# Operand sums of the output product made per head inside the memory attention, and one gate unit placed ahead of the spread of the key norms

## What is computed

```
# first stack, layers l = 0 and 1: attention to a memory of 256 rows, 4 heads of 256
q = rmsnorm(x, xa_ln[l]) @ xa_wq[l]
k = rmsnorm(mem, xa_mem_ln[l]) @ xa_wk[l]
v = rmsnorm(mem, xa_mem_ln[l]) @ xa_wv[l]
o = softmax(q @ k.T / 16) @ v            # per head
x = x + o @ xa_wo[l]

# second stack, layers A0 and A1: sliding window attention, 16 query heads and 4 key heads of 64
q, k, v, z = split(u @ a_w_in)
q = rope(rmsnorm_2(q, q_gain), pos)      # norms per head of 64
k = rope(rmsnorm_2(k, k_gain), pos)
o = window_attention(q, k, v, sinks)
y = (o * silu(z)) @ a_w_out
```

## Time and profile before

| what | value |
|---|---|
| median of 3 runs | 3629.98 us (3616.33 to 3632.56) |
| profiled execution, its own time | 3631.66 us |
| its span in the profile | 3629.8 us |
| mean granted TensorE clock | 0.976 of full |
| TensorE busy (matmuls) | 3461.8 us, 95% |
| VectorE busy | 1997.6 us, 55% |
| ScalarE busy | 716.1 us, 20% |
| GpSimd busy | 84.5 us, 2% |
| memory attention, layers mem0 and mem1 | about 523 to 555 and 1523 to 1555 us |
| gate stretch of the sliding layers | about 2099 to 2162 and 3432 to 3496 us |

### The profile page before, as it was taken

The page is one execution under the profiler, slowest core; times in us unless marked ns, Lnnn a source line. Parts: engine busy times, 40 slices in busy tenths (PEclk is TensorE's granted clock), DMA queues, the critical chain, the costliest instruction groups (busy, mean ns, idle before and its releaser), DMA issues.

```text
span 3629.8 us, 43978 instructions
## 1 busy us (share of the span) xinstructions
PE 3461.8 (95%) x16715; PEld 2727.9 (75%) x16715; DVE 1997.6 (55%) x4671; ACT 716.1 (20%) x1763; POOL 84.5 (2%) x100
## 2 busy tenths in 40 slices
PE   8987999999999999999999898999999999999988
PEld 3365688888854558888888765888887888887766
DVE  4353167554413783675544658644354656557566
ACT  2221011110012560111100125012212111121143
POOL 0000000000000000000000011000000000000110
PEclk9988999999999999999999999999999999999999
DMA  3100322222211003212222130222211222102311
GB/s 129 49 21 12 111 74 70 82 93 82 105 58 47 13 19 112 80 70 82 93 82 93 59 94 14 92 70 76 73 65 45 95 80 86 43 24 83 110 43 47
DMA packets 39367, 251.98 MB, mean 69 GB/s; under 512 B 5708, under 2 KB 5836, under 8 KB 11008
## 3 DMA queue, kind: packets, MB, share of 16 engines
q1 hardware_dynamic: 31616, 224.41, 17.5%
q10 hardware_dynamic: 4496, 11.89, 1.2%
q0 software_dynamic: 3056, 12.96, 1.1%
HBM read 240.58 MB, written 2.16 MB: 67 GB/s over the span
## 4 chain that ended last, share of the span: by engine, by line
PE 88%; DVE 8%; issue 2%; ACT 1%; DMA 1%; ACTq 0%; POOL 0%; POOLq 0%; DVEq 0%
PE PL L1213 26%; PE PX L1213 20%; PE PL L921 14%; PE PL L1561 4%; PE PL L1408 3%; PE PL L905 2%; PE PX L1670 2%; DVE SCR L2971 2%; PE PL L1326 1%; DVE SCR L2986 1%; PE PL L1586 1%; PE PX L1346 1%; PE PL L1713 1%; PE PX L931 1%; PE PL L1375 1%
## 5 line engine op out<-in xcount | busy, mean ns | idle before, releaser
L921 PE MATMUL PL<-xn,ring 128*128 128x264 f32 (+1 forms) x1600 | 506.6, 474 | 10.8 <-DVE xn L2365 10.2
L921 PEld LDWEIGHTS PL<-xn,ring 128*128 128x128 f32 x1600 | 305.8, 193 | 198.1 <-issue 165.4
L2408 DVE TENSOR_TENSOR Z<-PL,SCR 128x512 f32<-128x512 f32 (+3 forms) x104 | 63.8, 614 | 469.8 <-PE PL L921 372.0
L1213 PE MATMUL PL<-Z,ring 128*128 128x256 f32 (+1 forms) x1248 | 297.3, 388 | 10.5 <-DVE Z L3361 8.6
L1213 PEld LDWEIGHTS PL<-Z,ring 128*128 128x128 f32 x1248 | 240.7, 193 | 49.9 <-DVE Z L3361 10.1
L1213 PE MATMUL PL<-AUX,ring 128*128 128x256 f32 (+1 forms) x1056 | 243.9, 379 | 0.0
L1213 PEld LDWEIGHTS PL<-AUX,ring 128*128 128x128 f32 x1056 | 200.6, 190 | 27.6 <-DVE AUX L2739 0.2
L1213 PE MATMUL PL<-xn,ring 128*128 128x264 f32 (+1 forms) x864 | 204.1, 388 | 12.7 <-DVE xn L2365 11.5
L1213 PEld LDWEIGHTS PL<-xn,ring 128*128 128x128 f32 x864 | 165.7, 192 | 43.1 <-issue 12.4
L1841 ACT ACTIVATE SCR<-PL 128x256 f32<-128x256 f32 (+1 forms) x72 | 27.7, 384 | 737.1 <-PE PL L1213 737.1
L1213 PE MATMUL PX<-Z,AUX 128*128 128x264 f32 (+1 forms) x704 | 163.8, 384 | 2.7 <-DVE Z L3169 2.7
(11 more groups left out here) (515 smaller groups left out, 6055.2 us busy)
## 6 DMA issues: line engine op xcount, KB each, us to landing
ring<-w_tiles SPq DMA_DIRECT2D x212, 1024.0 KB, 4.8
Z<-Z ACTq DMA_DIRECT2D x16, 264.0 KB, 5.1
SCR<-head_rows POOLq DMA_DIRECT2D x16, 264.0 KB, 3.7
AUX<-norm_scratch POOLq DMA_DIRECT2D x8, 528.0 KB, 6.6
cst<-consts ACTq DMA_DIRECT2D x1, 2188.5 KB, 14.9
resid<-x ACTq DMA_DIRECT2D x4, 512.0 KB, 8.8
AUX<-mem POOLq DMA_DIRECT2D x2, 1024.0 KB, 5.1
AUX<-w_cmp POOLq DMA_DIRECT2D x1, 2048.0 KB, 10.6
```

Source lines behind the costliest of these rows:

```text
L921: mm = pe.matmul(PL[:, 2 * h + c, 0:e - a], ring[t % 2][:, k, P * h:P * h + P], src_block(name, k)[:, a:e], start=k == 0, stop=k == KB - 1)
L1213: mm = pe.matmul(ps, lhs(k), rhs(k), start=kc == 0 and k == 0, stop=kc == per - 1 and k == 3)
L2408: ins = dve.tensor_tensor(d, ps, f, ALU.mult)
```

## The change

Two edits.

1. The sums of `xo0` and `xo1` are made in four pieces, each as soon as its head's four outputs are copied out: in rounds 7, 11, 15 and 19 of VectorE's loop in the memory attention, right after the output copy. The block after the loop goes. The piece of the fourth head falls in the last round, where the whole block stood before.
2. In both sliding layers gate unit 2 stands ahead of the spread of the key norms, not behind it.

```diff
-        HEADS = {n: PAIRS if n in ("f10", ..., "A1_in") else ONE for n in QUADS}
+        HEADS = {n: PAIRS if n in ("f10", ..., "A1_in", "xo0", "xo1") else ONE for n in QUADS}
...
@@ TensorE, window @@
                 mm.then_inc(wq_tps, 1)
+                gate_part(2, 0, KB)
                 pe.wait_ge(pick_in, 16 * (i + 1))
                 for x in range(2):
...
                     mm.then_inc(wq_kbc, 1)
-                gate_part(2, 0, KB)
                 for u in range(3, 8):
...
@@ VectorE, attention @@
                     if n >= 4:
                         output(n - 4)
+                        if n % 4 == 3:
+                            pair_of = PAIRS[n // 4 - 1]
+                            dve.wait_ge(o_done, G0 + n - 3)
+                            sums_head("xo" + name[3], 0, pair_of)
+                            sums_tail("xo" + name[3], 0, pair_of)
...
@@ VectorE, the layers mem0 and mem1 @@
                     attention(layer)
-                    dve.wait_ge(o_done, group0[layer] + 16)
-                    sums_head(f"xo{l}", 0, (0, 4))
-                    sums_tail(f"xo{l}", 0, (0, 4))
                     quadrants(f"xo{l}")
```

More of the change, by code:

```diff
@@ L375, in build @@
         ONE, PAIRS = [(0, 4)], [(p, p + 1) for p in range(4)]
-        HEADS = {n: PAIRS if n in ("f10", "f11", "A0_out", "A1_out", "B_in", "C_in", "C_out", "A1_in") else ONE for n in QUADS}
+        HEADS = {n: PAIRS if n in ("f10", "f11", "A0_out", "A1_out", "B_in", "C_in", "C_out", "A1_in", "xo0", "xo1") else ONE for n in QUADS}
         HEADS["c_out"] = [(0, 3), (3, 4)]
```

## The result

| | before | changed |
|---|---|---|
| median of the runs (18 each) | 3628.26 us (3616.33 to 3632.56) | 3640.23 us (3633.44 to 3641.94) |
| ratio of the runs, 95% interval | | 1.0029 [1.0023, 1.0036] |
| profiled execution: its own time, span | 3631.66, 3629.8 us | 3641.88, 3640.1 us |
| mean granted TensorE clock | 0.976 | 0.975 |

The change makes the kernel slower by 12.0 us by the medians. The ratio gives 0.0029 x 3628 = 10.5 us (8.3 to 13.1). The forecast was +5.4 us.

What follows compares the result with a forecast made beforehand. TensorE was taken as the bound, so only its gaps count. Edit 1 at +5.0 us and edit 2 at +0.4 sum to +5.4; from the median 3629.98 this gives 3635.4 us, range 3617 to 3647.

Steps and rivals of the forecast that it cites:

- What bounds: Whole kernel: TensorE holds 88% of the chain; the wide sums after the attention are already hidden, xo waits for an output copy.
- the walk of the waits: Memory attention: VectorE's added sums delay TensorE at scores 12, scores 15 and turn 15; xo 2.5 us later per layer.
- One sign: Memory attention, new profile: a TensorE wait of 0.4 to 1.3 us ahead of scores 12 and 15 and turn 15.
- the same copy: Sliding layers: gate unit 2 waits for VectorE's copy of unit 0, so the gap stays as long; +0.4 us in all.
- The sign for unit 3: Sliding layers, new profile: unit 3 starts within 1 us of where it did against the copy of gate unit 0.
- the clock is the unknown: Half clock behind the gate gaps: the same 5.0 us in all; bounds -5.0 and +6 us.
- No cost: Behind edit 2 in the sliding layers: later keys, ropes and copies have room on VectorE, 3.57 us idle before unit 3's copy.
- The slack: Rival, memory attention: VectorE catches up in its idle half microseconds and xo starts when it did; 3630.4 us, chance 0.14.
- breaking up: Rival, start of xo: it starts sooner by at most its 0.58 us gap per layer; 3629.2 us, chance 0.06.
- the gate unit: Rival, sliding layers: unit 2 fills the gap, winning 3.3 us per layer and 5.0 of half clock; 3623.4 us, chance 0.12.
- VectorE did not become the bound: Rival, attention: all 4.65 us per layer land on TensorE and the clock falls too; 3651.9 us, chance 0.08.

Runs made afterwards that it cites:

- E1: Kernel before with edit 1 alone (sums per head), gate order as before: 3636.09 us against 3627.67, ratio 1.0019.
- E5: Kernel before with edit 1 alone and the weight sums moved from rounds 8 and 9 to 4 and 5: 3627.09 us against 3629.41, ratio 0.9999.
- E6: Kernel before with weight sums in rounds 4 and 5, two heads' sums in rounds 7 and 11, two behind the loop: 3632.99 us against 3629.41, ratio 1.0006.
- E7: Kernel before, wide sums kept, plus four dummy sums of 256 columns in rounds 7, 11 and 15: 3634.48 us against 3629.41, ratio 1.0016.
- E8: The changed kernel run once more beside new runs of the kernel before: 3638.38 us against 3631.28, ratio 1.0017.
- E2: Kernel before with edit 2 alone (gate unit 2 ahead of the spread), sums as before: 3629.38 us against 3627.67, ratio 1.0003.
- E3: Kernel before with VectorE's copies of gate units 0 and 1 moved up, behind ropes 1 and 4: 3618.57 us against 3627.67, ratio 0.9967.
- E10: Kernel before with the first matmul of xo0 issued 4 times more, a delay of 1.83 us: ratio 1.0013.
- E12: Kernel before with the first matmul of xo0 issued 12 times more, a delay of 5.29 us: ratio 1.0017.

## Why the prediction was right and where it was off

The measured time, 3640.23 us, lies in the range of 3617 to 3647, and the change is below half a per cent, as forecast. The likeliest value was 4.8 us too low. The range was drawn for the scatter of the runs and would have held a loss of nothing as well; what speaks for the mechanism is the stages, not the whole time.

- **What bounds.** Right. The tail's wide sums were hidden: `xo`'s gap of 0.58 us and its releaser are the same with edit 1 and without (changed kernel, E1, E5, E6, E7), m6 does not wait, and E6 shows that half of the sums early win nothing.
- **Edit 1, the walk of the waits.** Right in place, order and size: 0.71, 1.10, 2.23 and 2.58 us where 0.7, 1.0 to 1.1, 2.2 to 2.4 and 2.5 were written. A head cost 1.60 us where 1.55 stood. E7 shows that the load alone does it, E5 that the weight sums in rounds 8 and 9 had taken the room. One sign was missed in part: ahead of scores 15 no wait of 0.4 us or more is marked. They start 548.67 - 547.49 = 1.18 us after the values before them, where 0.89 is the rule in the rounds without a wait (545.52 to 546.41), so some 0.3 us were lost there.
- **Edit 2, the same copy.** Right: +0.42 us in the two gate stretches where +0.4 stood, the gap 3.50 and 3.44 us, its releaser L2408. The sign for unit 3 failed: in A0 its copy comes 2141.42 - 2121.79 = 19.6 us after the end of the copy of unit 0, where it came 2133.33 - 2115.14 = 18.2 before, 1.4 us later instead of under 1. The half clock behind the gap cost 10.15 - 7.12 = 3.0 us here and 8.90 - 7.12 = 1.8 in A1, where 1.9 and 3.1 had been read before: the same 4.8 to 5.0 in all, dealt the other way. The room on VectorE was smaller than said, too: 0.31 us of idle is left before the copy of unit 3, of the 3.57.
- **The mis-sized term.** It was "the clock is the unknown ... with a gap of the same length I take the same 5.0 us". The clock was priced at the two gate gaps alone, and there the price held. What was left out is every other place of the kernel at which the clock may fall or not, such as the wait in layer B: 3.80 us before, 6.86 after, in both profiles. It was put at nothing without a reason, and "No cost" for what comes after edit 2 is open for the same cause. The changed kernel's 18 runs had a mean clock of 0.9755, those of before 0.9764 to 0.9774 in the four later batches. At 3.0 us per 0.001 that is 2.7 to 5.7 us, about the 4.9 between 5.6 (the edited stages) and 10.5 (the ratio). This is a sum that fits, not a cause that is shown, and it compares runs that were not made side by side; side by side with E8 the clocks were 0.9761 and 0.9764, which is 0.9 us.
- **The rivals.** The slack did not absorb edit 1 (35.05, not 32.47 us), breaking up did not pay (E6), the gate unit did not fill the gap by itself (E2), and VectorE did not become the bound: the losses were 2.6 us per attention and not 4.65, and no half clock came inside it. The Trainium skill's advice on breaking up instructions (Perfetto Trace Analysis, Optimizing Scalar/DVE Operations) has its condition in the same sentence, that the engine is causing bubbles elsewhere. Here no bubble ended with a sum, and the pieces made new ones.
- **The Trainium skill on the clock** (TensorE: Matmul & The Clock Gate, What's actually happening): that activity releases the half clock agrees with the half clock behind both gaps. E3 shows the other side in A0, where 1.9 us came back beyond the 3.3 of the gap once TensorE did not stop. In A1 only 1.4 of 3.1 us came back: the clock fell behind the spread though TensorE was busy all along (0.50 in 3445 to 3448).

**What stays open.** Where the first comparison's 10.5 us (8.3 to 13.1) go beyond the 5.6 of the edited stages. E8's runs cost only 6.2 us (2.9 to 9.8), which holds the 5.6, so part of it may be scatter between sets of runs. Part of it may be edit 2's after all, through the clock in layer B. E10 to E12 shifted unchanged code and did not settle it; they did not reproduce the fall there.

## What to carry to other kernels

Before work is moved ahead of a wait, read who ends that wait: here it was an output copy in one place and a gate copy in the other, and neither edit touched them. The edit that did, the gate copies moved up on the releasing engine (E3), won 12 us by the ratio (8.0 to 15.6) and 9 by the medians against the kernel before. Work moved from a covered tail into a loop costs whatever exceeds the loop's slack, and that slack could be walked here to a tenth of a microsecond, the operations that already use it included.

## What the runs showed of the hardware

- Behind one and the same wait of 2.69 us the same 16 matmuls took 3.80 us at 2.4 GHz in eleven profiles, and 5.34 (E2) or 6.86 us (the changed kernel, twice) with all or part at 1.2 GHz. The trace of one kernel cannot say what such a wait costs in another.
- TensorE's clock can fall to half while TensorE is busy without a stop: 0.50 in 3445 to 3448 of E3, with 3.00 of 3.00 us busy, behind the turned reciprocals and the spread of the key norms.
- Runs of one and the same kernel on one chip differ by up to 19 us (E12: 3620.30 to 3639.34) with 0.005 of mean granted clock. The first 520 us, the same code everywhere, differed by 16 us between profiles. A later stage of the same code differed by 4 us (967.44 to 971.49). So a difference of 1 to 3 us in unchanged code, in one profile each, can't be put down to the edit.
- Four sums of 256 columns cost 1.60 us inside the attention. Four such sets are 6.4 us against 4.76 for the four wide sums: made in four pieces each, these sums cost a third more VectorE time.
